# A PEER router that works key side by key side over all tiles of tokens, in place of tile by tile

## What is computed

```python
PEER_HEADS, N_KEYS, PEER_TOPK = 8, 128, 16
q  = (x @ wq).reshape(T, PEER_HEADS, 2, 128)            # T = 640
s1 = einsum('thd,hnd->thn', q[:, :, 0], k1)              # two sides of keys, 128 keys each
s2 = einsum('thd,hnd->thn', q[:, :, 1], k2)
v1, i1 = top_k(s1, 16)
v2, i2 = top_k(s2, 16)
cand = (v1[..., :, None] + v2[..., None, :]).reshape(T, PEER_HEADS, 256)
cidx = (i1[..., :, None] * N_KEYS + i2[..., None, :]).reshape(T, PEER_HEADS, 256)
best, pos = top_k(cand, 16)
idx   = take_along_axis(cidx, pos, axis=-1)
gates = softmax(best, axis=-1)
```

## Time and profile before

| what | value |
|---|---|
| median of 3 runs | 4546.27 us (4543.84 to 4549.11) |
| the profiled execution | 4545.1 us, its span 4543.0 us |
| TensorE matmul busy | 3937.9 us, 87% |
| VectorE (DVE) busy | 3575.8 us, 79% |
| ScalarE (ACT) busy | 1480.8 us, 33% |
| GpSimd (POOL) busy | 1950.7 us, 43% |
| mean granted TensorE clock | 0.94 |

### The profile page before, as it was taken

The page is one execution under the profiler, slowest core; times in us unless marked ns, Lnnn a source line. Parts: engine busy times, 40 slices in busy tenths (PEclk is TensorE's granted clock), DMA queues, the critical chain, the costliest instruction groups (busy, mean ns, idle before and its releaser), DMA issues. The chain is left out here.

```text
span 4543.0 us, 79900 instructions
## 1 busy us (share of the span) xinstructions
PE 3937.9 (87%) x29354; PEld 3271.4 (72%) x29354; DVE 3575.8 (79%) x7332; ACT 1480.8 (33%) x2779; POOL 1950.7 (43%) x1687
## 2 busy tenths in 40 slices
PE   6679999978948899999999579689479999999994
PEld 1246666655936899999999478359368899999994
DVE  4325666654899799999999865648997999999998
ACT  1024444432226333333333232022263333333332
POOL 0001111111359466666666500313584666666665
PEclk8889999989979999999999789899799999999997
DMA  9520000012005999999999522120069999999996
GB/s 371 212 77 17 19 19 19 17 58 108 2 1 165 378 406 400 406 407 406 391 394 396 220 83 76 70 92 2 1 176 385 402 399 407 406 406 390 393 397 229
DMA packets 394136, 1044.93 MB, mean 230 GB/s; under 512 B 37367, under 2 KB 168695, under 8 KB 391672
## 3 DMA queue, kind: packets, MB, share of 16 engines
q0 software_dynamic: 147456, 536.94, 30.0%
q1 hardware_dynamic: 219448, 488.74, 28.9%
q10 hardware_dynamic: 27008, 16.25, 1.2%
HBM read 986.26 MB, written 55.54 MB: 229 GB/s over the span
## 5 line engine op out<-in xcount | busy, mean ns | idle before, releaser
L884 PE MATMUL bank<-h_parts,u_parts 128*128 128x384 f32 x6144 | 1118.7, 337 | 39.8 <-DVE u_parts L979 36.6
L884 PEld LDWEIGHTS bank<-h_parts,u_parts 128*128 128x128 f32 x6144 | 1083.2, 189 | 61.9 <-issue 36.9
L894 PE MATMUL bank<-v_parts,gg_parts 128*128 128x512 f32 x4608 | 1102.1, 393 | 11.4 <-DVE v_parts L999 11.2
L894 PEld LDWEIGHTS bank<-v_parts,gg_parts 128*128 128x128 f32 x4608 | 864.2, 189 | 186.5 <-issue 14.5
L862 POOL DMA_INDIRECT late<-in_peer_v,rows_idx x512 | 619.5, 1210 | 197.8 <-issue 151.5
L968 DVE SCALAR_TENSOR_TENSOR late<-late,yT 128x1024 f32<-128x1024 f32 x512 | 659.8, 1290 | 34.6 <-DMA late<-in_peer_v,rows_idx 20.0
L854 POOL DMA_INDIRECT late<-in_u_rows,rows_idx x256 | 348.0, 1359 | 304.0 <-DVE yT L962 293.8
L935 ACT ACTIVATE gg_parts<-late 128x384 fp32r<-128x384 f32 x256 | 133.7, 522 | 1034.6 <-DVE late L989 1029.1
L958 DVE TENSOR_TENSOR u_parts<-hT,u_parts 128x1024 fp32r<-128x1024 f32 x256 | 311.3, 1216 | 44.2 <-ACT u_parts L932 44.2
L488 PE MATMUL bank<-hT,late 128*128 128x128 f32 x2560 | 315.6, 278 | 8.7 <-PEq L60 8.7
L999 DVE TENSOR_TENSOR v_parts<-yT,v_parts 128x1024 fp32r<-128x1024 f32 x256 | 311.2, 1216 | 0.0
(11 more groups left out here) (380 smaller groups left out, 5659.0 us busy)
## 6 DMA issues: line engine op xcount, KB each, us to landing
yT<-in_peer_v SPq DMA_DIRECT2D x256, 512.0 KB, 6.5
hT<-in_peer_u SPq DMA_DIRECT2D x256, 512.0 KB, 8.1
w_modt<-in_w_mod SPq DMA_DIRECT2D x24, 2048.0 KB, 18.2
late<-gates SPq DMA_DIRECT2D x168, 192.0 KB, 7.8
late<-in_peer_wq SPq DMA_DIRECT2D x32, 512.0 KB, 12.1
gates<-late SPq DMA_DIRECT2D x2, 8192.0 KB, 30.4
gates<-gates_sb SPq DMA_DIRECT2D x2, 8192.0 KB, 30.6
w_raw<-in_hy_w_in SPq DMA_DIRECT2D x24, 512.0 KB, 3.6
```

The costliest lines, as they stand in the source:

```text
L884: mm = pe.matmul(m.bank[j % 2][:, 0:TD], us[:, j % 2, a, k, :], hs[:, b, k, :], start=(k == 0 and i == 0), stop=(k == KD - 1 and i == 2))
L894: mm = pe.matmul(yb[t][c][:, :], gs[:, j, a, t * P:(t + 1) * P], vs[:, j % 2, b, c * BANK:(c + 1) * BANK], start=(first and i == 0), stop= ...
```

## The change

The loops of the router run over sides. Each side's queries are made for the four latent tiles with matmuls of 512 columns and for the context tile with 128; its scores for all five tiles follow at once. ScalarE copies them into one of 8 slots (HELD). VectorE takes a head at a time: `top16` over 2 sides x 5 tiles, then the pairs of the 5 tiles, now 3 x 16 and 13 x 4, so 100 (WIDE = 3). Places, comparisons and sums of the softmax are done for groups of heads (GROUPED: 2, 2, 2, 1, 1). GpSimd gets the conversion of the indices and the last product of the softmax beside the multiplying and folding of the first four groups; VectorE does these of the last group. The nine transposes of `sel` and the expert numbers of the sparse tiles stand at the end of the block.

```diff
-WIDE = 4
+WIDE = 3
 NARROW = 4
+HELD = 8
+GROUPED = ((0, 2), (2, 2), (4, 2), (6, 1), (7, 1))
+SHARED = len(GROUPED) - 1
...
+                for n in range(SIDES):
+                    queries(n)
+                    scores(n)
+                    if n in (4, 5):
+                        rows(n - 4)
...
+                for t in range(NSP, TT):
+                    for a in range(3):
+                        mm = pe.transpose(m.bank[3 + t][:, a * P:(a + 1) * P], sel[:, t, a, :], m.ident[:, :])
+                    mm.then_inc(s["pk_tr"], 1)
...
+                def indices(g):
+                    a, heads = first(g)
+                    pool.wait_ge(s["pk_ab"], g + 1)
+                    pool.tensor_copy(idxf[:, :, 0:heads], idx[:, g % 2, :, 0:heads]).then_inc(s["pk_conv"], 1)
+                    pool.wait_ge(s["pk_conv"], g + 1)
+                    pool.wait_ge(s["pk_hot"], g + 1)
+                    times_index(pool, g, 0)
+                    link(times_index(pool, g, 1))
                     for half in (8, 4, 2):
+                        link(fold(pool, g, half))
+                    choose(pool, g, 0)
+                    choose(pool, g, 1).then_inc(s["pk_dec"], 1)
...
+                for g in range(SHARED):
+                    indices(g)
+                    if g >= 1:
+                        gates(g - 1)
+                gates(SHARED - 1)
...
+                def keys_of(h, sides):
...
+                    dve.wait_ge(s["pk_sc"], 2 * h + sides[-1] + 1)
+                    if a == 0 and g >= 2 and sides[0] == 0:
+                        dve.wait_ge(s["pk_conv"], g - 1)
+                    rows = [(side, t) for side in sides for t in range(TT)]
...
+                def places(g):
...
+                    dve.tensor_tensor(ab[:, 1, 0:n], posf[:, 0:n], corner[:, 1, 0:n], ALU.subtract).then_inc(s["pk_ab"], 1)
+                    dve.wait_ge(s["pk_ab"], g + 1)
+                    if g >= 1:
+                        dve.wait_ge(s["pk_dec"], min(g, SHARED - 1))
+                    for side in range(2):
+                        ins = dve.tensor_tensor(hot(g, side), ab[:, side, 0:n].unsqueeze(2).broadcast_to([P, n, TOPK]),
+                                                m.iota[:, 0:TOPK].unsqueeze(1).broadcast_to([P, n, TOPK]), ALU.is_equal)
+                    ins.then_inc(s["pk_hot"], 1)
...
+                for g, (h0, heads) in enumerate(GROUPED):
+                    for h in range(h0, h0 + heads):
...
+                            keys_of(h, [0, 1])
+                        pairs_of(h)
+                    differences(g)
+                    places(g)
+                    if g >= 1:
+                        sums(g - 1)
```

More of the change, by code:

```diff
@@ new lines, in peer_route, with first, chosen @@
+        norm = buf(ctx, nc, "norm", P, 2, PH, TT)
+        s = s | sems(ctx, nc, "pk_chain", "pk_found", "ps_q", "ps_qsb", "ps_s", "pk_sc", "pk_scfree", "pk_dif", "pk_exp", "pk_norm", "pk_gated", "pk_lastgate",
+                     "pk_ab", "pk_hot", "pk_conv", "pk_dec", "pk_lastdec", "pk_row", "pk_rows", "pk_tr", "pk_out")
+        def first(g):
+            h0, heads = GROUPED[g]
+            return (0 if g < SHARED else 1), heads
+        def chosen(g, side):
+            h0, heads = GROUPED[g]
+            return sel[:, :, side, h0 * TOPK:(h0 + heads) * TOPK].rearrange("p t (h k) -> p h t k", k=TOPK)
@@ new lines, in hot, with times_index, fold @@
+        def hot(g, side):
+            a, heads = first(g)
+            return eq[:, side, a * HEAD:(a + heads) * HEAD]
+        def times_index(eng, g, side):
+            a, heads = first(g)
+            e = hot(g, side).rearrange("p (r q) k -> p r q k", q=TOPK)
+            index = idxf[:, side, a:a + heads].rearrange("p h t k -> p (h t) k").unsqueeze(2).broadcast_to([P, heads * TT, TOPK, TOPK])
+            return eng.tensor_tensor(e, e, index, ALU.mult)
+        def fold(eng, g, half):
+            a, heads = first(g)
+            e = eq[:, :, a * HEAD:(a + heads) * HEAD]
+            return eng.tensor_tensor(e[:, :, :, 0:half], e[:, :, :, 0:half], e[:, :, :, half:2 * half], ALU.add)
@@ new lines, in choose, with share @@
+        def choose(eng, g, side):
+            a, heads = first(g)
+            e = hot(g, side).rearrange("p (h t q) k -> p h t q k", h=heads, t=TT)
+            return eng.tensor_tensor(chosen(g, side), e[:, :, :, :, 0], e[:, :, :, :, 1], ALU.add)
+        def share(eng, g, a, n, out):
+            h0, heads = GROUPED[g]
+            to = out.rearrange("p t (h k) -> p h t k", k=TOPK)[:, h0:h0 + heads]
+            return eng.tensor_tensor(to, gate[:, h0:h0 + heads, a:a + n], norm[:, 1, h0:h0 + heads, a:a + n].unsqueeze(3).broadcast_to([P, heads, n, TOPK]), ALU.mult)
@@ L478, in _ @@
             def _(pe):
[L479 to L522, removed]
+                def queries(n):
+                    if n % 4 == 0:
+                        pe.wait_ge(s[f"ps_w{n // 4}"], 64)
+                    for k in range(KD):
+                        mm = pe.matmul(m.bank[n % 2][:, :], S.wq[:, n, k, :], m.hT[:, k, T_CTX:T], start=(k == 0), stop=(k == KD - 1))
+                    mm.then_inc(s["ps_q"], 1)
+                    for k in range(KD):
+                        mm = pe.matmul(m.bank[2][:, n % 2 * P:(n % 2 + 1) * P], S.wq[:, n, k, :], m.hT[:, k, 0:T_CTX], start=(k == 0), stop=(k == KD - 1))
+                    mm.then_inc(s["ps_q"], 1)
@@ new lines, in scores @@
+                def scores(n):
+                    pe.wait_ge(s["ps_qsb"], 2 * n + 1)
+                    if n == 0:
+                        pe.wait_ge(s["ps_keys"], 16)
+                    if n >= 2:
+                        pe.wait_ge(s["pk_sc"], n - 1)
+                    for t in range(1, TT):
+                        mm = pe.matmul(m.bank[4 + n % 2][:, (t - 1) * P:t * P], S.qT[:, n % 2, t * P:(t + 1) * P], S.keys[:, n, :], start=True, stop=True)
+                    mm.then_inc(s["ps_s"], 1)
+                    pe.wait_ge(s["ps_qsb"], 2 * n + 2)
+                    pe.matmul(m.bank[3][:, n % 4 * P:(n % 4 + 1) * P], S.qT[:, n % 2, 0:P], S.keys[:, n, :], start=True, stop=True).then_inc(s["ps_s"], 1)
@@ new lines, in rows @@
+                def rows(t):
+                    if t >= 1:
+                        pe.wait_ge(s["pk_rows"], t)
+                    for k in range(KD):
+                        mm = pe.transpose(m.bank[6 + k // 4][:, (k % 4) * P:(k % 4 + 1) * P], m.hT[:, k, t * P:(t + 1) * P], m.ident[:, :])
+                    mm.then_inc(s["pk_row"], 1)
+                for n in range(SIDES):
[3 more added lines that the diff above has]
+                        rows(n - 4)
@@ L524, in _ @@
             @block.scalar
             def _(act):
[L526 to L539, removed]
@@ L555, in _, with query_copies @@
[L555 to L562, removed]
+                def query_copies(n):
+                    act.wait_ge(s["ps_q"], 2 * n + 1)
+                    act.activation(S.qT[:, n % 2, T_CTX:T], m.bank[n % 2][:, :], ACT.Copy).then_inc(s["ps_qsb"], 1)
+                    act.wait_ge(s["ps_q"], 2 * n + 2)
+                    act.activation(S.qT[:, n % 2, 0:T_CTX], m.bank[2][:, n % 2 * P:(n % 2 + 1) * P], ACT.Copy).then_inc(s["ps_qsb"], 1)
@@ new lines, in _ @@
+                for n in range(SIDES):
+                    query_copies(n)
+                    score_copies(n)
+                    if n in (4, 5):
+                        row_copies(n - 4)
+                    if n in (5, 9, 13):
+                        exponents(n // 4 - 1)
+                exponents(3)
+                exponents(4)
+                for t in range(NSP, TT):
+                    act.wait_ge(s["pk_tr"], t - NSP + 1)
+                    act.activation(selT[:, :, (t - NSP) * P:(t - NSP + 1) * P], m.bank[3 + t][:, 0:3 * P].rearrange("p (a t) -> p a t", a=3), ACT.Copy).then_inc(s["pk_out"], 1)
@@ L566, in _ @@
                 link = linker(pool, s["pk_found"])
[L567 to L574, removed]
-                    for half in (8, 4, 2):
[L576 to L583, removed]
@@ L657, in _ @@
-                normalize(TT - 1)
-                decode_last()
-                dve.wait_ge(s["pk_gated"], TT)
+                def keys_of(h, sides):
+                    g = min(h // 2, 3) if h < PH - 1 else SHARED
+                    a = h - GROUPED[g][0]
+                    dve.wait_ge(s["pk_sc"], 2 * h + sides[-1] + 1)
+                    if a == 0 and g >= 2 and sides[0] == 0:
+                        dve.wait_ge(s["pk_conv"], g - 1)
+                    rows = [(side, t) for side in sides for t in range(TT)]
+                    top16(dve, link, [sc[:, (2 * h + i) % HELD, t] for i, t in rows], [sc2[:, i, t] for i, t in rows],
+                          [vals[:, i, t] for i, t in rows], [idx[:, g % 2, i, a, t] for i, t in rows])
@@ new lines, in _ @@
+                last = SHARED
+                link(dve.tensor_copy(idxf[:, :, 1], idx[:, last % 2, :, 0]))
+                dve.wait_ge(s["pk_hot"], last + 1)
```

(11 more changed lines are left out.)

180 lines of the change are left out of this document (84 added, 96 removed).

## The result

The changed kernel takes 4569.31 us (median of 5 runs, 4562.24 to 4574.22), the kernel before beside it 4546.13 (5 runs): a ratio of 1.0056 [1.0043, 1.0069], 23.2 us slower. The forecast was +25.4.

What follows compares the result with a forecast made beforehand. VectorE was taken to bound the router block; per layer -4.2 - 7.0 + 20.6 + 1.9 + 1.4 = +12.7 us, twice 25.4 on 4545.1, with 1.2 for the median: 4572 us. Range for 8 in 10: 4551 to 4582.

Steps and rivals of the forecast that it cites:

- The bound: Router block: VectorE works last and bounds it, so what VectorE gains or loses there, the kernel does.
- Turns with GpSimd: VectorE's sums of pairs behind groups 0, 1 and 2 wait for GpSimd's folds: +20.6 us a layer.
- the second wait: After the first sum, GpSimd's next fold gets in and runs 2.9 us, so the second sum of pairs waits too.
- Waits for scores: VectorE's idle time for scores inside its stretch: 10.2 us in place of 17.2, so -7.0 a layer.
- VectorE's work: VectorE's lists, pairs, places, comparisons, softmax and last decode in the router: -4.2 us a layer.
- Conversion and softmax beside the comparisons: GpSimd's conversion and last softmax fall beside VectorE's comparisons and last products: +1.9 us a layer, an estimate.
- End of the block: Behind VectorE's last choice: nine transposes in place of three, +1.4 us a layer.
- The late exponent: ScalarE's wait for an exponent delays sides 14 and 15 by ten-odd us; VectorE wants them later, so no cost.
- start: Start of VectorE's stretch: side 0 ready and first MAX8 at 1121.4, as in the kernel before.
- rival of no wait: VectorE's sums of pairs don't wait for GpSimd, as L686's row has it: -8.7 us a layer, 4529; chance 9%.
- rival of one wait: Second sum follows the first before GpSimd's next fold: 11.8 in place of 20.6, +3.9 us a layer, 4554; chance 14%.
- late scores: Sides 14 and 15 over 20 us later, head 7 waits: at most 5 us a layer more, 4582; 5%, shared with dearer instructions.

Runs made afterwards that it cites:

- hold: The changed kernel with GpSimd's folds started only when both sums of pairs of the next head are done; 4534.27 us, 0.9976 of the kernel before.
- onefold: The changed kernel without GpSimd's second and third fold, so the chosen indices are wrong; 4554.09 us, 1.0018 of the kernel before.
- firstpair: The changed kernel with rounds of one head, except that heads 0 and 1 share the first; 4550.17 us, 1.0007 of the kernel before.
- late4096: The kernel before with two more GpSimd instructions of 2048 elements in each round, whose result nobody reads; 4581.77 us, ratio 1.0077.
- oneinput: The changed kernel with GpSimd's folds replaced by one-input multiplications by 1, so the chosen indices are wrong; 4557.23 us, 1.0022 of the kernel before.

## Why the prediction was right

- **The bound.** VectorE's stretch set the router, and both layers moved alike (+11.7, +11.6). Right.
- **Turns with GpSimd.** 20.6 forecast, 21.1 found; 5.12, 4.67, 4.61 for L662 (4.3 to 4.9 forecast, so the first is a little over) and 3.08 for L665 (3.2). hold, which moves only GpSimd's start of the folds, takes away 17.1 of the 21.1 and shows where the other 4.0 went; onefold and firstpair confirm the second wait and the tie to a double round. So this term is shown, not only argued.
- **Waits for scores.** -7.0 forecast, -6.9 found. The side's pace was 9.8 us, as forecast.
- **VectorE's work.** -4.2 forecast, -5.3 found. The five sums of the softmax were put at 0.55 and take 0.37 to 0.48 (behind group 1 from 1236.62 to 1237.09): 0.5 of the difference. The comparisons, put at 5.6 and 2.95, come to 5.5 and 2.81: 0.6. The 2.81 is measured (1341.33 to 1344.14); the 5.5 is an estimate from L637 in the kernel before, 4.41 us for 2048 elements a side.
- **Conversion and softmax beside the comparisons.** 1.9 forecast, 0.9 found: a pair of comparisons beside it takes 5.74 us (1177.95 to 1183.69) in place of the 5.5 above, once in each full group. Most of the waiting is GpSimd's: L617 takes 3.1 us for 320 elements beside the comparisons, where L641, a conversion of 256 elements behind them, takes 0.40.
- **End of the block.** +1.4 forecast, +1.6 found.
- **The late exponent** did delay sides 14 and 15 and cost nothing: they were ready at 1285.4 and 1296.5, and head 7's lists start at 1320.8. VectorE had no fourth wait.

The total is 11.7 a layer against 12.7 in the sum. The mechanism is as forecast; the nearness of the total is in part luck, since work and conversion came out 1.1 and 1.0 lower and start, turns and end 0.2, 0.5 and 0.2 higher.

The rival of no wait falls with L662, the rival of one wait with L665, late scores with the six waits in all. What the prediction had not seen is that VectorE's instructions with one input (conversions, L681) wait as well; here it made no odds, since none of them met a fold in the changed kernel.

## What to carry to other kernels

When a round of work is split between VectorE and GpSimd, lay the two timelines beside each other and look at which VectorE instructions fall into GpSimd's long ones: here sums with two inputs and a conversion waited until it was over, and two in a row waited twice, while MAX8 and the searches did not (ten lists took 12.2 us beside GpSimd's products, and 12.2 with GpSimd idle). The size of a round decides this more than its total work does: eight rounds of one head, with more instructions in all, beat the five rounds of the change, three of them double, by 43 us (4526 against 4569), of which 10 are a shorter wait for scores. Where a collision can't be avoided, let GpSimd wait a moment (1.7 to 2.1 us in hold) rather than start a long instruction just ahead of VectorE.

## What the runs showed of the hardware

- Turns were taken both ways: where such instructions of both engines met, one of each went alternately (folds 8.54 us in place of 8.02 in late4096, while L615, L600 and L623 waited).
- A conversion and an integer shift of VectorE, with one input each, waited for a GpSimd fold: 3.91 us in place of 0.29 (late4096), 2.85 in place of 0.19 (hold).
- GpSimd's multiplication of one input by a constant was slower than its addition of two, 6.70 against 5.56 us for 2560 elements of the same strided table; no VectorE instruction is the reason, since in group 3, where both of VectorE's sums came behind it, 1280 elements took 3.45, the same pace.
- L686 and L753, with two inputs, never waited beside a busy GpSimd (192 times, at most 0.43 us). That GpSimd's instruction there has one input is not enough as a reason: in oneinput a multiplication with one input held up L663 for 5 us. What the reason is stays open.
